# Latent-attention heads of a hybrid encoder: one VectorE subtraction moved from behind the third row maximum to ahead of the first

## What is computed

```python
def mla_attention(p, q_norm_g, w_q_b, kv_norm_g, w_kv_b, cos, sin):
    c_q, c_kv, k_pe = jnp.split(p, [MLA_Q_RANK, MLA_Q_RANK + MLA_KV_RANK], -1)
    q = (rms_norm(c_q, q_norm_g) @ w_q_b).reshape(B, T, MLA_HEADS, 64 + 32)
    kv = (rms_norm(c_kv, kv_norm_g) @ w_kv_b).reshape(B, T, MLA_HEADS, 64 + 64)
    q_nope, q_pe = jnp.split(q, [64], -1)
    k_nope, v = jnp.split(kv, [64], -1)
    q_pe = apply_rope(q_pe, cos[:, None, :], sin[:, None, :])
    k_pe = apply_rope(k_pe, cos, sin)
    q = jnp.concatenate([q_nope, q_pe], -1)
    k = jnp.concatenate([k_nope, jnp.broadcast_to(k_pe[:, :, None, :], ...)], -1)
    ...
    s = jnp.einsum('bqhd,bkhd->bhqk', q_blk, k) * scale
    prob = jax.nn.softmax(s, axis=-1)
    return jnp.einsum('bhqk,bkhd->bqhd', prob, v)
```

## Time and profile before

| | before |
|---|---|
| median of 3 runs | 1568.75 us (1568.62 to 1570.34) |
| the profiled execution | 1570.64 us |
| its span, first to last instruction | 1568.8 us |
| mean granted TensorE clock | 0.999 of full speed |
| PE busy | 1520.7 us, 97% |
| DVE busy | 1043.6 us, 67% |
| ACT busy | 636.4 us, 41% |
| POOL busy | 345.8 us, 22% |

### The profile page before, as it was taken

The page is one execution under the profiler, slowest core; times in us unless marked ns, Lnnn a source line. Parts: engine busy times, 40 slices in busy tenths (PEclk is TensorE's granted clock), DMA queues, the critical chain, the costliest instruction groups (busy, mean ns, idle before and its releaser), DMA issues.

```text
span 1568.8 us, 25838 instructions
## 1 busy us (share of the span) xinstructions
PE 1520.7 (97%) x10160; PEld 1101.0 (70%) x10160; DVE 1043.6 (67%) x1503; ACT 636.4 (41%) x1178; POOL 345.8 (22%) x356
## 2 busy tenths in 40 slices
PE   6999999999999999999999999999999999999998
PEld 5788775645555556777754467888888888888786
DVE  7424589778666576666557489775555555689877
ACT  6212246656444444444430225433333333334553
POOL 0900014123410038888810140220000000000000
PEclk9999999999999999999999999999999999999999
DMA  6131010010000010001041012332221211756322
GB/s 245 54 147 53 20 54 14 7 28 13 12 24 12 7 32 3 2 2 29 2 182 74 0 54 69 127 122 86 81 81 54 57 62 44 275 195 207 115 68 108
DMA packets 29001, 110.70 MB, mean 71 GB/s; under 512 B 3568, under 2 KB 6096, under 8 KB 26720
## 3 DMA queue, kind: packets, MB, share of 16 engines
q1 hardware_dynamic: 28432, 103.97, 19.4%
q0 software_dynamic: 464, 5.28, 0.8%
HBM read 89.36 MB, written 18.92 MB: 69 GB/s over the span
## 4 chain that ended last, share of the span: by engine, by line
PE 71%; issue 12%; DVE 9%; POOL 5%; ACT 2%; DMA 1%; DVEq 0%; SPq 0%; POOLq 0%; ACTq 0%
PE psum L2908 24%; PE psum L2925 12%; PE psum L2832 7%; PE psum L2578 4%; PE psum L2605 3%; PE psum L2496 2%; PE psum L2612 2%; PE psum L2515 1%; PE psum L2466 1%; POOL arena L852 1%; POOL arena L854 1%; PE psum L2806 1%; PE psum L2701 1%; PE psum L2719 1%; PE psum L2715 1%
## 5 line engine op out<-in xcount | busy, mean ns | idle before, releaser
L1987 DVE TENSOR_TENSOR part_lo<-arena,part_hi 128x512 fp32r<-128x512 f32 x154 | 117.8, 768 | 77.3 <-ACT part_hi L1268 77.1
L2908 PE MATMUL psum<-h_hi,part_hi 128*128 128x512 f32 x616 | 165.7, 391 | 1.1 <-ACT arena L1316 0.7
L2908 PE MATMUL psum<-h_lo,part_hi 128*128 128x512 f32 x616 | 164.7, 389 | 0.0
L2908 PE MATMUL psum<-h_hi,part_lo 128*128 128x512 f32 x616 | 164.6, 389 | 0.0
L1268 ACT ACTIVATE part_hi<-arena 128x512 fp32r<-128x512 f32 x154 | 95.9, 628 | 132.6 <-PE psum L2908 114.9
L2908 PEld LDWEIGHTS psum<-h_hi,part_hi 128*128 128x128 f32 x616 | 115.2, 188 | 26.7 <-ACT arena L1316 1.1
L2908 PEld LDWEIGHTS psum<-h_lo,part_hi 128*128 128x128 f32 x616 | 115.7, 188 | 24.1
L2908 PEld LDWEIGHTS psum<-h_hi,part_lo 128*128 128x128 f32 x616 | 115.7, 188 | 24.0
L918 POOL TENSOR_TENSOR arena<-arena,consts 128x512 f32<-128x512 f32 x64 | 81.9, 1300 | 135.2 <-ACT arena L1169 134.6
L2832 PE MATMUL psum<-arena 128*128 128x512 f32 x256 | 110.5, 592 | 0.0
L1657 DVE TENSOR_REDUCE stats<-psum 128x1 f32<-128x1024 f32 x64 | 77.8, 1216 | 44.9 <-PE psum L2496 44.7
(11 more groups left out here) (329 smaller groups left out, 3025.7 us busy)
## 6 DMA issues: line engine op xcount, KB each, us to landing
arena<-in_w_gate SPq DMA_DIRECT2D x22, 512.0 KB, 3.7
arena<-in_w_up SPq DMA_DIRECT2D x22, 512.0 KB, 3.7
arena<-in_w_down SPq DMA_DIRECT2D x22, 512.0 KB, 3.6
arena<-in_w_down SPq DMA_DIRECT2D x11, 1024.0 KB, 5.0
arena<-in_w_in SPq DMA_DIRECT2D x15, 512.0 KB, 3.5
arena<-act_spill SPq DMA_DIRECT2D x12, 512.0 KB, 7.0
act_spill<-arena SPq DMA_DIRECT2D x10, 512.0 KB, 6.0
arena<-in_x SPq DMA_DIRECT2D x8, 512.0 KB, 8.1
```

Of the source, the lines that this page charges most:

```text
L1987: v.tensor_tensor(lo, raw[:, at:at + HALF], hi, ALU.subtract).then_inc(part_lo, 1)
L2908: mm = pe.matmul(bank({2: z, 3: y, 5: y}.get(p, x)), w[:, P * k:P * k + P], h[k // 2][:, HALF * (k % 2):HALF * (k % 2) + HALF], start=(fre ...
```

## The change

One line of `beside`, in VectorE's program. The low part of the next head's rotated queries is placed at kt = 0, which comes before row maximum 0, in place of kt = 3, which comes after row maximum 2. The condition under which it runs, its operands and its semaphores are the same. It applies wherever `beside` places it, that is in the stretches of heads 1 to 6; the copies for heads 0 and 1 are issued elsewhere and stay.

```diff
@@ -1783,7 +1783,7 @@
                     def beside(kt):
                         if kt == 2 and (before is not None or b):
                             invert(*((i, 0) if b else (before, 1)))
-                        elif kt == 3 and (before is not None or b) and not (last and b):
+                        elif kt == 0 and (before is not None or b) and not (last and b):
                             turned_queries_lo(*((i + 1, 0) if b else (i, 1)))
                         if before is None and (b, kt) in SCANS_AT:
                             scan(SCANS_AT[b, kt])
```

## The result

The changed kernel takes 1578.99 us (median of 6 runs, 1574.42 to 1581.92) against 1569.34 us before (6 runs, 1568.62 to 1570.61): a ratio of 1.0052, 95% interval 1.0042 to 1.0062. That is slower, as forecast, but by 9.6 us where 4.3 us were forecast, and outside the range, which ended at 1575.2. A second series gave 1577.76 against 1571.24 us, 1.0044 (1.0027 to 1.0062). So the loss is 6.5 to 9.6 us.

The account below looks back on a forecast made before the run. TensorE, busy 97% of the span, was taken as the bound; delays of 1.69, 1.44, 1.58 and three times 0.05 us (4.86) less 0.58 gave 4.3 us on 1568.75: 1573.1 us, range 1569.8 to 1575.2.

Parts of the forecast that it names:

- the mechanism of the stall: Ahead of row maximum 0, the moved instruction waits for GpSimd's L898, making row maximum 0 about 1.7 us late in stretches 1 to 3.
- The lock: Two-SBUF-input VectorE and SBUF-reading GpSimd instructions wait for each other's whole instruction; a wait of 1.66 us at the new place.
- The size of the stall: TensorE delay after slack in stretches 1 to 6: 1.69, 1.44, 1.58 and three times 0.05 us, less 0.58 us.
- The three new waits: TensorE idle ahead of L2496, waiting for row maximum 0 in stretches 1 to 3, about 1.6 us each.
- The 0.58 us swallowed in stretch 1: Stall of guards 5 and 6 on row maxima 4 and 5 in stretch 1, taken up by the later TensorE: 0.58 us.
- so I carry the delay through unchanged: Behind the heads, everything hangs on TensorE's last values, so the 4.3 us delay reaches the end in full.
- a second wait for L900: Rival: in three stretches VectorE also waits for GpSimd's L900, 1.32 us more each; 8.3 us slower, 1577.0 us, chance 0.05.

Follow-up runs that it names:

- The kernel with a third of the filling: Changed kernel with the first product of scores 2 (two matmuls, 0.47 us) issued twice in stretches 0 to 6: 1576.17 against 1570.18 us before.
- its filled form: Changed kernel with the six matmuls of scores 2 issued twice in stretches 0 to 6: 1578.93 against 1570.64 us before.

## Why the prediction was wrong

- **Place, sign and the mechanism of the stall** were right. The moved instruction lies ahead of row maximum 0 in stretches 1 to 6, meets L898 in three of them and takes 2.85, 2.62 and 2.73 us; it ends 1.08 to 1.09 us after L898. L900 takes 2.05 us and L908 is back at 2.38 us, as forecast. The lock held over a wait of 1.76 us (358.25 to 360.01), more than twice what the rows of before showed. The rule of the Trainium skill, "SBUF — State Buffer", section "Who interferes with whom", on which this leant, agrees with these rows.
- **The size of the stall** was right: 1.69 - 0.58, 1.44, 1.58 and three times 0.05 us were worked out, and the second series shows 1.15, 1.44, and in stretch 3 2.95 us with one fall in it. The kernel with a third of the filling shows 1.15, 1.43 and 1.59 us.
- **The three new waits** were forecast as about 1.6 us of TensorE's idle time each and are 1.44, 1.20 and 1.32 us. The delays that they stand for are as forecast.
- **The 0.58 us swallowed in stretch 1** was right within 0.05 us (1.69 - 1.15 = 0.54).
- **The step that failed** is "so I carry the delay through unchanged": the sum, and the range with it, put a change of TensorE's clock at nothing without giving a reason. The forecast took it that idle time costs its own length. Three waits of 1.2 to 1.44 us each come with a chance of a fall to half the clock, at 1.35 to 1.46 us apiece in the stretch lengths. In the profiled execution two falls behind the new waits and one in stretch 0 cost 4.2 us, as much as the stall. The trace of before would not have given the term: its 1.82 us wait in stretch 0 was followed by full clock. One profile that shows no fall is no proof that none comes.
- **The rival that came nearest in its number**, 1577.0 us by a second wait for L900, is near in its number only. L1642 ended at 361.10, while L900 (from 360.12) was under way and was itself the one held up.
- **The width**: the changed kernel's runs are 7.5 us apart, those of before 2.0 in the same series (and 5.6 over all series). A range taken from the spread of before was bound to be too narrow once the change itself makes the clock's falls likely.
- What stays open: the fall in stretch 0 of the changed kernel's first profile has nothing to do with the moved instruction, since all of the work there is the same. Six of the other kernels here have falls in stretch 0 too, and the kernel before, with a mean clock of 0.9975 over 64 executions against the 0.9989 of its profile, must have falls in many of them. So part of the 9.6 us of the first series is chance; the second series, at 6.5 us, fits that.

## What to carry to other kernels

A VectorE instruction with two SBUF inputs that is put ahead of something TensorE waits for has to be checked against what GpSimd starts at the same moment: idle time on VectorE is no cover if GpSimd has just begun an instruction on SBUF. When the sum gives TensorE a new wait of a microsecond or more in a kernel like this one, add a term for the clock, with a wide range, or keep TensorE's wait short; here 0.5 us of repeated matmuls in the wait cost nothing there, and the clock stayed up in the three stretches with it. And a place behind a long block of TensorE's own work, like the old one here, gives real cover.

## What the runs showed of the hardware that was not expected

- TensorE's granted clock fell from 1.00 to 0.50 behind single waits of 1.15 to 1.44 us in an otherwise full stream of matmuls (5 of 13 times), behind 2.0 us in 4 of 6, and never behind 0.58 to 0.97 us (0 of 12). In stretch 0 it fell behind 5 of 14 waits of 1.1 us and 2 of 7 of 1.8 us. In stretch 1 of the changed kernel it was low from about 362.6 to 366.0.
- It fell after some waits and not after others of the same length in the same program, so that the runs of one kernel lie up to 7.5 us apart while those of its filled form lie within 0.8 us.
- The lock makes GpSimd wait as well: L900 took 2.05 instead of 1.2 us, and L908 4.22 instead of 2.38 us behind a scan. A tensor_scalar of 128 x 8 with one SBUF input waited for GpSimd too (L1709, 1.14 instead of 0.16 us).
